# State-space decays: the constant mask as the matmul's weight, the step sizes streamed in two parts for four heads at once

## The reference, cut to what matters

```python
dt = jax.nn.softplus(dt + dt_bias)            # (256, 32): step sizes
a = -jnp.exp(a_log)
# ssd_chunked:
a_cum = jnp.cumsum(dt * a, axis=2)            # within each chunk of 128
xdt = x * dt[..., None]
seg = a_cum[:, :, :, None] - a_cum[:, :, None, :]
decay = jnp.exp(jnp.where(causal, seg, -jnp.inf))
cb = jnp.einsum('bcign,bcjgn->bcijg', cm, bm)
y_diag = jnp.einsum('bcijg,bcijgr,bcjgrp->bcigrp', cb, decay, xdt)
```

## Time and profile before

| | us |
|---|---|
| median of 3 runs | 935.45 (935.07 to 939.02) |
| the profiled execution's own time | 936.12 |
| its span, first to last instruction | 934.3 |
| PE busy | 899.6 (96%) |
| DVE busy | 678.2 (73%) |
| ACT busy | 510.9 (55%) |
| POOL busy | 81.4 (9%) |
| chain that ended last: share of PE / DVE / ACT / issue | 63% / 6% / 6% / 3% |
| the stage's first and last L917 record | 638.0 / 708.1 |

### The profile page before, as it was taken

The page is one execution under the profiler, slowest core; times in us unless marked ns, Lnnn a source line. Parts: engine busy times, 40 slices in busy tenths (PEclk is TensorE's granted clock), DMA queues, the critical chain, the costliest instruction groups (busy, mean ns, idle before and its releaser), DMA issues.

```text
span 934.3 us, 14617 instructions
## 1 busy us (share of the span) xinstructions
PE 899.6 (96%) x5801; PEld 786.6 (84%) x5801; DVE 678.2 (73%) x968; ACT 510.9 (55%) x732; POOL 81.4 (9%) x83
## 2 busy tenths in 40 slices
PE   6999999999999989999999899999999998999998
PEld 5998988988888769999988699988888786878777
DVE  6688737856868678898854668787686777776665
ACT  7863332243535376665643565765565666577553
POOL 6002402300000000000000000007320000000000
PEclk9999999999999989999999999999999999999999
DMA  9543222122555455565555454552323544532231
GB/s 310 171 149 105 92 91 90 47 92 90 195 188 179 149 168 181 189 208 189 183 190 197 153 172 147 185 180 90 112 82 123 176 151 153 204 105 91 91 116 64
DMA packets 80979, 136.63 MB, mean 146 GB/s; under 512 B 3957, under 2 KB 46545, under 8 KB 80912
## 3 DMA queue, kind: packets, MB, share of 16 engines
q1 hardware_dynamic: 78800, 131.17, 42.1%
q0 software_dynamic: 2112, 4.53, 1.6%
HBM read 134.64 MB, written 1.05 MB: 145 GB/s over the span
## 4 chain that ended last, share of the span: by engine, by line
PE 63%; DVE 6%; ACT 6%; issue 3%; DMA 1%; DVEq 0%; ACTq 0%
PE bank L443 18%; PE bank L445 17%; PE bank L444 17%; PE bank L432 3%; DVE lower L1903 2%; ACT upper L1333 2%; PE bank L1112 1%; PE bank L917 1%; PE bank L925 1%; PE bank L1096 1%; DVE arena L2456 1%; ACT arena L1819 1%; DMA loaded<-in_ffn_w_up 1%; DMA loaded<-in_ple_gate_w 1%; ACT arena L1432 1%
## 5 line engine op out<-in xcount | busy, mean ns | idle before, releaser
L1903 DVE TENSOR_TENSOR lower<-loaded,upper 128x2048 fp32r<-128x2048 f32 x122 | 278.6, 2287 | 123.8 <-ACT upper L1333 121.7
L1333 ACT ACTIVATE upper<-loaded 128x2048 fp32r<-128x2048 f32 x122 | 231.9, 1903 | 115.3 <-PE bank L445 99.0
L443 PE MATMUL bank<-xT_upper,upper 128*128 128x256 f32 (+1 forms) x664 | 186.5, 281 | 2.7 <-DVE lower L1895 1.6
L444 PE MATMUL bank<-xT_lower,upper 128*128 128x256 f32 (+1 forms) x664 | 185.0, 279 | 0.0
L445 PE MATMUL bank<-xT_upper,lower 128*128 128x256 f32 (+1 forms) x664 | 184.9, 278 | 0.0
L443 PE MATMUL bank<-upper,xT_upper 128*128 128x512 f32 (+1 forms) x360 | 146.7, 407 | 4.6 <-DVE lower L1903 3.4
L445 PE MATMUL bank<-upper,xT_lower 128*128 128x512 f32 (+1 forms) x360 | 139.9, 389 | 0.0
L444 PE MATMUL bank<-lower,xT_upper 128*128 128x512 f32 (+1 forms) x360 | 139.3, 387 | 0.0
L443 PEld LDWEIGHTS bank<-xT_upper,upper 128*128 128x128 f32 (+1 forms) x664 | 125.1, 188 | 4.1 <-DVE lower L1895 1.8
L444 PEld LDWEIGHTS bank<-xT_lower,upper 128*128 128x128 f32 (+1 forms) x664 | 125.3, 189 | 0.2
L445 PEld LDWEIGHTS bank<-xT_upper,lower 128*128 128x128 f32 (+1 forms) x664 | 125.2, 189 | 0.1
(11 more groups left out here) (349 smaller groups left out, 1167.9 us busy)
## 6 DMA issues: line engine op xcount, KB each, us to landing
loaded<-in_w_in SPq DMA_DIRECT2D x26, 1024.0 KB, 5.1
loaded<-in_ffn_w_up SPq DMA_DIRECT2D x22, 1024.0 KB, 5.1
loaded<-in_ssm_in_w SPq DMA_DIRECT2D x20, 1024.0 KB, 5.2
loaded<-in_ffn_w_down SPq DMA_DIRECT2D x11, 1024.0 KB, 4.9
loaded<-in_ssm_out_w SPq DMA_DIRECT2D x8, 1024.0 KB, 4.9
loaded<-in_ple_gate_w SPq DMA_DIRECT2D x8, 1024.0 KB, 5.0
loaded<-in_attn_in_w SPq DMA_DIRECT2D x8, 1024.0 KB, 5.2
loaded<-in_w_branch_ret SPq DMA_DIRECT2D x4, 1024.0 KB, 4.9
```

The lines of the kernel that those rows point to most:

```text
L443: mm(out, a[0], b[0], start=start, stop=False)
L444: mm(out, a[0], b[1], start=False, stop=False)
L1333: A(part(upper, PARTS, n), part(loaded, LOADS, n), ACT.Copy).then_inc(uppers, 1)
L1903: TT(part(lower, LOADS, n), part(loaded, LOADS, n), part(upper, PARTS, n).bitcast(F32), sub) \
```

## The change

The roles of the two operands are exchanged. PE's weight is now the constant mask `masks[:, 1]` (fp32r), and what is streamed is `incl` times the step sizes, for four heads in one matmul of 512 columns. fp32r keeps fewer bits than fp32, so the step sizes are split into a rounded upper part and the rest (`adt_upper`, `adt_lower`), and two matmuls add up in PSUM: where there were four fp32 matmuls of 128 columns, there are two fp32r matmuls of 512. POOL makes both streamed operands, `steps[:, 0]` and `steps[:, 1]`, with one instruction each, so two a step for one before. `steps` fills the room that had been `later`'s two buffers, so there is one buffer: `later_steps(z)` now waits for PE's step z-1. DVE makes the two parts once, with two small instructions. POOL's skips are put elsewhere: two behind `later_steps(1)`, two behind `later_steps(2)`.

```diff
+        steps = nc.alloc_sbuf_tensor_at("steps", [P, 2, 4, P], F32R, offset=consts_at + 4 * where[ROOM][0])
...
-                pe.wait_ge(sem("later_steps"), z + 1)
                 ps = take(pe, ("bc", z), 4 + z % 2)
-                for e in range(4):
-                    last = mm(ps[:, P * e:P * e + P], later[:, z % 2, e, :], const("incl"), start=True, stop=True)
+                for m in range(2):
+                    pe.wait_ge(sem("later_steps"), 2 * z + m + 1)
+                    last = mm(ps[:, :].rearrange("p (a b) -> p a b", a=4), masks[:, 1, :], steps[:, m, :, :],
+                              start=(m == 0), stop=(m == 1))
...
-                if z >= 2:
-                    full(pool, ("bc", z - 2))
-                pool.tensor_tensor(later[:, z % 2, :, :], masks[:, 1, :].bitcast(F32).unsqueeze(1).broadcast_to([P, 4, P]),
-                                   adt[:, n, hd:hd + 4].unsqueeze(2).broadcast_to([P, 4, P]), ALU.mult) \
-                    .then_inc(sem("later_steps"), 1)
-
-            pool.wait_ge(sem("masks_ready"), 1)
-            pool.wait_ge(sem("adt_ready"), 1)
+                if z:
+                    full(pool, ("bc", z - 1))
+                for m, part_ in enumerate((adt_upper.bitcast(F32), adt_lower)):
+                    pool.tensor_tensor(steps[:, m, :, :], const("incl").unsqueeze(1).broadcast_to([P, 4, P]),
+                                       part_[:, n, hd:hd + 4].unsqueeze(2).broadcast_to([P, 4, P]), ALU.mult) \
+                        .then_inc(sem("later_steps"), 1)
+
+            pool.wait_ge(sem("adt_split"), 2)
             later_steps(0)
-            later_steps(1)
             pool.wait_ge(sem("rowp_landed"), 96)
             pool.wait_ge(sem("xd_ready"), 3)
...
-            for g in range(2):
-                skip(g, 0)
-                skip(g, 1)
+            later_steps(1)
+            skip(0, 0)
+            skip(0, 1)
             later_steps(2)
+            skip(1, 0)
+            skip(1, 1)
...
                 TT(adt[:, :, :], dtv[:, :, :], bc(arow.unsqueeze(1), P, 2, 32), mul).then_inc(sem("adt_ready"), 1)
+                ve.wait_ge(sem("adt_ready"), 1)
+                ve.tensor_copy(adt_upper[:, :, :], adt[:, :, :]).then_inc(sem("adt_split"), 1)
+                ve.wait_ge(sem("adt_split"), 1)
+                TT(adt_lower, adt[:, :, :], adt_upper[:, :, :].bitcast(F32), sub).then_inc(sem("adt_split"), 1)
```

More of the change, by code:

```diff
@@ L33 @@
 LEVELS = 7
+ROOM = "off0"
 WHOLE = 5
@@ L168, in sem @@
             return sems[name]
+        consts_at = (nc.sbuf_base + 31) // 32 * 32
         consts = sb("consts", [P, ncols])
+        steps = nc.alloc_sbuf_tensor_at("steps", [P, 2, 4, P], F32R, offset=consts_at + 4 * where[ROOM][0])
         loaded_at = (nc.sbuf_base + 31) // 32 * 32
@@ L183, in build @@
         xT = (sb("xT_upper", [P, KT, T], F32R), sb("xT_lower", [P, KT, T], F32R))
+        small_at = (nc.sbuf_base + 31) // 32 * 32
         small = sb("small", [P, 1408])
+        adt_upper = nc.alloc_sbuf_tensor_at("adt_upper", [P, 2, 32], F32R, offset=small_at + 4 * 520)
         posi = sb("posi", [P, 4], I32)
@@ L292, in build @@
         dtT = lora[:, 1, 0:T]
-        later = consts[:, where["off0"][0]:where["off0"][0] + 8 * P].rearrange("p (a b c) -> p a b c", a=2, b=4)
+        adt_lower = sm(584, 2, 32)
         ang, cosd, sind = sm(520, 4, 32), sm(648, 4, 64), sm(904, 4, 64)
```

## The result

The changed kernel took 944.2 us (median of 5 runs, 943.29 to 946.09) where the kernel before, in the same comparison, took 935.41 (934.09 to 939.02): 1.0081 times as long, 95% interval 1.0063 to 1.010. The medians lie 8.8 us apart, which alone would be 1.0094; the ratio, taken over the runs, is 7.6 us, and its interval 5.9 to 9.4. The forecast was 946.7, rival A 943.8.

The account below looks back on a forecast made before the run. PE was taken to bound the kernel, with DVE close behind. 936.12 + 8.3 for the stage + 3.0 for the clock = 947.4 us for the profiled execution, 946.7 for the median; 8 in 10 range 937 to 951.5.

Parts of the forecast that it names:

- rival A: Whole stage: POOL and DVE serialised as forecast, but no clock loss; 943.8 us, chance 0.26.
- The turns at the port: DVE instructions reading two SBUF operands and POOL instructions never overlap; each waits for the other's end, in turns.
- the walk: Hand simulation of the engine queues: POOL 1.03 us, DVE 0.62 or 2.25 for a split, turns taken; stage 8.3 later.
- PE's saving: Sixteen spreads on PE go from 0.89 to 0.46 us each, 6.9 us saved, bounds 5.8 to 7.4.
- Part 1: Stage start: POOL's operands are late, PE waits 5.1 us at steps 2 and 3; spread(3) ends 3.3 us later.
- Part 2: Up to the first group turn: PE waits for POOL at steps 5 and 7; group_turns(0,1) comes 5.0 us later.
- Part 3: DVE's run through group 1 takes 3.2 us longer, PE idles 5.2; the turn at 689.94 comes 8.0 later.
- Part 4: Steps 13 to 15 and behind the last spread: turns at 710.01 and 725.55 come 8.4 and 8.2 us later.
- Part 5: PE's idle time before the late group-1 turn drops the clock to half for seven us, adding 3.0 us.
- B: Only the stage start costs, POOL's later instructions are hidden: 934 to 938.5 us, chance 0.14.
- C: Operand pairs are ready in time from step 2, PE keeps its 6.9 us: 928.5 to 932, chance 0.08.
- D: POOL's rounded-output instruction takes 1.10 us or more and the clock also falls at the start: 950 and above, chance 0.10.

Follow-up runs that it names:

- b_pool_twice: Kernel before, with POOL making each step's operand twice (32 instructions) and PE's spread waiting for the second; two buffers and fp32 matmuls kept: 1.0055.
- b_pe_quick: Kernel before with two 512-column fp32r matmuls a step, both streaming POOL's one operand; two buffers, old order, sums wrong: 0.9962.
- a_two_buffers: Changed kernel with a second buffer for both streamed operands and step 1 made ahead of the skips: 1.0055.
- b_one_buffer: Kernel before with one buffer for POOL's operand and the changed kernel's order of skips; one POOL instruction a step, fp32 matmuls: 1.0014.
- a_one_pool: Changed kernel with POOL making only the upper operand (16 instructions), streamed twice by PE, lower part left out: 0.9957, 932.8 us.

## Why the prediction was right, and where it was off

The sign, the mechanism and the places were right. The sum was 11.3 us, where the medians say 8.8, the ratio 7.6 and the trace, within the stage, 7.4. So the terms were too large by more than the medians show; some 1.1 us of the profiled execution come from ahead of any changed instruction and brought the time nearer to the forecast by luck. The sizes are taken part by part, with the trace's values.

- *The turns at the port* held: a waiting instruction waits out the other engine's one. The Trainium skill (page SBUF — State Buffer, section Who interferes with whom) has the same rule, and the trace agrees. The 115 ns at the end of a wait, which the same page of the Trainium skill (section A bandwidth-pool intuition that's wrong) gives for a transfer whose descriptors GpSimd writes, don't show here: POOL's waiting instruction at 644.23 ended at 647.33, 0.90 us after the split's end at 646.43, and takes 1.03 alone. What was a little too dear in the walk is the `weigh` between two POOL instructions, 0.62 us for 0.46 in the rows.
- *PE's saving.* Spread(1) to the start of the next block is 0.45 us, as taken, and the worth of 3.8 for PE's side alone was measured as 3.6.
- *Part 1, the start:* +3.3 forecast, +3.0 found. But not as written. I had 2.3 us of waiting at step 2 and 2.75 at step 3. Step 2 waited 2.67, the clock fell to 1.2 GHz right behind it, and PE did the next block at half speed until 652.8, so that step 3 found its operands ready. POOL set the pace either way. It began 0.6 us later than in the walk (640.23, less 1.1, for 638.5) and needed 13.4 us for 14.4.
- *Part 2:* +5.0 forecast at group_turns(0,1), +3.2 found. This term was mis-sized. Step 5 didn't wait (1.1 forecast), step 7 waited 0.76, not 2.2, and 0.78 us went to `carried(0)` waiting for DVE, which I had not seen. From step 3's second operand to step 5's POOL took 8.9 us (653.67 to 662.61), not 6.2 + 4.1: `gated` came only behind the pair, and each `weigh` held POOL up for less than its length. An error in who asks first moves a turn by 1 us; I carried it as exact.
- *Part 3:* DVE's run 3.2 us longer forecast, 3.0 found; waits within it 4.2 forecast (the six terms written there add up to 4.1), 4.0 found; PE's idle time 5.2 forecast, 4.65 found. The 5.2 doesn't follow from the terms beside it: 1.36 + 8.0 - 5.0 + 1.7 is 6.1, unless PE waits some 0.8 us for POOL in between, which the part doesn't name. The trace has such a wait, 0.84 us at step 9.
- *Part 4:* +0.4 and -0.2 forecast; +1.1 to the next turn with the clock in it, +0.1 behind.
- *Part 5, the clock:* it fell as said, but cost 1.6 us, not 3.0: this is the other mis-sized term. The forecast took the whole stretch at 0.50 for work. In the earlier trace rows nearly all of it was: the clock fell at 341.3, half a us before PE's turn, and came back at 348.1. Behind the turn here it fell 3.4 us ahead of PE's work and came back 3.4 us into it. The other end, 2.8 us for 3.8 us at half speed, was wrong as a sum: 3.8 us at half speed cost 1.9 at most.

Of the rivals, B falls (`b_pool_twice`: the later instructions do cost), C falls (PE waited for POOL at the very step named), A was nearest in time, but its reason is wrong, as the clock did fall; D's slower POOL instruction wasn't found (1.03 with a rounded output), though its fall of the clock at the start was.

Where the expected gain went, as ratios to the kernel before:

| | 16 POOL instructions | 32 POOL instructions |
|---|---|---|
| slow spreads, two buffers | 1 (the kernel before) | 1.0055 (`b_pool_twice`) |
| quick spreads, two buffers | 0.9962 (`b_pe_quick`) | 1.0055 (`a_two_buffers`) |
| slow spreads, one buffer | 1.0014 (`b_one_buffer`) | not run |
| quick spreads, one buffer | 0.9957 (`a_one_pool`) | 1.0081 (the changed kernel) |

With 32 POOL instructions and two buffers the quick spreads are worth nothing: 1.0055 with and without them. So POOL's second instruction costs 5 us beside the slow spreads and 9 beside the quick ones, since it also takes back what PE had gained. The one buffer costs next to nothing with 16 instructions (+1.3 and -0.5 us, both within the intervals). With 32 it costs perhaps 2.4 more, with intervals that overlap: there more of POOL's delays are also PE's (its waits for POOL add up to 4.3 us in the changed kernel's trace and to 1.1 with two buffers).

## What to carry to other kernels

An engine at 9% busy is not free: in these traces a GpSimd instruction and a VectorE instruction with two operands in SBUF took turns, so an instruction added on GpSimd is paid for by VectorE, and by whoever waits for VectorE. Before adding GpSimd work, look at the longest unbroken run of VectorE that something waits for, and count the two-operand SBUF reads in it. If the work must be there, give VectorE one operand from PSUM: here that was worth 5 us, as much as the second GpSimd instruction cost in the kernel before. And a faster TensorE gains nothing where the next engine is already as late as that: count what both engines need before the point where they meet.

## What the runs showed of the hardware that I had not expected

- 1.78 and 0.89 us of idle time of PE, 0.5 us apart, were followed by a granted clock of 0.50 from about 649.4 to 652.8. In `b_pe_quick` and in `a_one_pool` a single wait of 2.22 us ahead of group_turns(1, 0) was followed by 0.50 as well, from 688.3 to 691.7 and from 691.0 to 694.4; the 1.36 us of the kernel before were not.
- The clock can fall while PE is still idle. Around the turn at 697.22 it was 0.50 from 693.8 to 700.6, of which 3.4 us were work; around 341.88 in the trace before it was 0.50 from 341.3 to 348.1, of which 6.2 us were work. What such a stretch costs depends on how much of it is idle time.
- A `weigh` with one operand in PSUM took 685 ns on average beside 32 POOL instructions, against 1041 with both in SBUF; 0.68 us is what it takes undisturbed.
- The time at which the stage begins differs from trace to trace (its first `ac` matmul between 605.8 and 613.4 us), though next to nothing ahead of it was changed. A profile of one execution is to be compared from a row inside it, not from the span.
